# Ten weight slots with the expert loop written out, and expert 0's rows picked on TensorE, in a two-layer mixture-of-experts decoder

## The chip, the core and the metric

The kernel runs on one core of a Trainium2 chip. The metric is the device time of one execution in microseconds (us); the median of three executions is quoted. The engines are TensorE (PE; weight loads are listed as PEld), VectorE (DVE), ScalarE (ACT), GpSimd (POOL) and SyncE (SP). A name with a q behind it (SPq, ACTq) is that engine's sequencer issuing a DMA.

## What is computed

520 tokens (512 of a prompt, 8 decode tokens) of width 1024 pass two layers. Each layer has a mixer (short gated convolution in layer 0, RG-LRU recurrence in layer 1), a layer norm, a mixture of 32 experts in 4 groups, and a second layer norm. All is float32. The part around the change is the mixture:

```python
def hier_moe(x, w_group, w_expert, w_gate, w_up, w_down):
    gp = jax.nn.softmax((x2 @ w_group), axis=-1)
    g = jnp.argmax(gp, axis=-1)                        # one group of 4 per token
    el = (x2 @ w_expert).reshape(t, N_GROUPS, EXP_PER_GROUP)
    el = jnp.take_along_axis(el, g[:, None, None], axis=1)[:, 0]
    vals, idx = lax.top_k(softmax(el), TOP_K)          # two experts of its 8
    ...
    hmid = jax.nn.silu(xb @ w_gate[e]) * (xb @ w_up[e])
    out = hmid @ w_down[e]
```

Every expert's three matrices (1024x512, 1024x512, 512x1024) are read once per layer: 192 units of 2 MB, some 400 MB in all.

## The kernel before

**Weights.** `ring` holds RING = 9 slots of 2 MB. Every load has a position: 0 to 7 are layer 0's input weights, 8 and 9 its output weights, 10 to 105 its experts (gate, up and down of expert e at 10+3e, 11+3e, 12+3e), and so on for layer 1. Position p goes into slot p % RING. SP issues the loads in order (L427; L421 and L423 for the one unit that is loaded in two halves); ahead of each, `room(pos)` waits on the semaphore `freed` until the unit RING positions earlier has been used. PE raises `freed` in `project` (gate's first use, which releases the down unit before it, and its last), and with the first transposition of `turn_rows` (up's slot). For expert 0 the gate slot is released in two halves.

**Experts.** An expert handles up to 64 token rows; further rows go into overflow blocks after expert 30. PE per expert: `project(0)` with gate and `project(1)` with up (L894, 32 matmul instructions each), `turn_rows` for the next expert's rows (L880), `turn_hidden` (L916), `down` (L926, 16 instructions). A float32 matmul is two instructions. ACT applies Silu (L1208) and copies the result out (L1213); DVE multiplies (L1665), copies the turned hidden rows (L1668) and applies the norm's gain and bias to the turned token rows (L1646, L1649). POOL gathers each expert's token rows out of `x1` in DRAM with an indirect DMA (L567) into one of UNROLL = 3 buffers `xg`, and scatters the results to `yrows` (L574) from one of three buffers `yo`. The first HEAD = 6 experts and the last two are written out; the 24 between run in a loop of 8 trips of 3 on SP, PE, ACT.

**Routing, before expert 0.** The order in a layer is: the mixer's last products (L726), the logits (L778, L825), turned to tokens (L833); tokens turned to rows (`turn_token`, L787); DVE computes the variance and the logits, picks the group (L1546 to L1551), then twice the best expert (L1555 to L1561), and writes `picked` (L1562). Meanwhile ACT normalises the five token tiles `xk` (L1192), and ACT and POOL store them to `x1` (L1187, L558). PE counts ranks (L842, L845), DVE makes the one-hots `rowhot` (L1575), PE turns them into row numbers (L855), DVE writes `idx` (L1287), POOL gathers expert 0's rows (L567). PE sums the destinations (`destinations`, L863), runs six products as a warm-up (`warm`, L650) and waits for the gather; then `turn_rows`, DVE's `first_rows` (L1657, L1661), and `project(0)` of expert 0. `overflow` on DVE (blocks of experts with over 64 rows) follows `first_rows`.

**After the experts.** SP reads the scattered rows back into the ring slots of expert 30 (`rows_back`, L437), DVE and PE add them, the second layer norm follows, and layer 1 begins with its input weights (L444).

## Time and profile before

| | us |
|---|---|
| median of 3 executions (1460.77 to 1463.67) | 1462.91 |
| profiled execution, span from first to last instruction | 1458.7 |
| PE busy in it | 1295.1 (89%) |
| DVE busy | 467.0 (32%) |
| ACT busy | 204.4 (14%) |
| POOL busy | 145.9 (10%) |
| DMA moved | 475.39 MB, mean 326 GB/s |

The profile page has a row for each engine and resource in 40 equal slices of the span (36.5 us each). A chain of work follows the last instruction back to what released it at each step. A busy PE is not PE at its peak, since the ends of pipelined matmuls are modelled; so the question at each stretch is which wait ended last.

### The profile page before, as it was taken

How to read it: one execution, taken by the hardware profiler on the slowest of the kernel's cores; microseconds unless marked ns; L12 is line 12 of the kernel's file. 1: busy time of each engine (PE TensorE's matmuls, PEld its weight loads, DVE VectorE, ACT ScalarE, POOL GpSimd, SP SyncE). 2: the span in 40 equal slices, each digit the busy share in tenths (PEclk: the TensorE clock that was granted, in tenths of full speed). 3: DMA queues.
4: the chain of work that ended last, by engine and by line, in shares of the span. 5: the costliest groups of instructions: out<-in, count | busy, mean ns of one | idle time of the engine just before them, and what ended most of it. 6: DMA issues, size and time to landing. Idle time of an engine off the chain costs nothing.

```text
span 1458.7 us, 20116 instructions
## 1 busy us (share of the span) xinstructions
PE 1295.1 (89%) x8446; PEld 888.8 (61%) x8446; DVE 467.0 (32%) x966; ACT 204.4 (14%) x332; POOL 145.9 (10%) x165
## 2 busy tenths in 40 slices
PE   7999997999998878878899999989999878878886
PEld 6888876666664444444478887766666444444452
DVE  5666414322321111111245755261232111111116
ACT  1000012001000000000155563120100000000011
POOL 0000001111111111110000000021111111111101
PEclk9999998999999999999999999989999999999999
DMA  9930363899999999999995113269999999999995
GB/s 271 311 144 0 136 270 117 331 424 424 422 424 427 423 424 426 423 425 426 385 323 231 58 59 141 93 233 425 424 421 424 425 422 427 424 424 427 422 400 203
DMA packets 101037, 475.39 MB, mean 326 GB/s; under 512 B 18902, under 2 KB 53718, under 8 KB 66669
## 3 DMA queue, kind: packets, MB, share of 16 engines
q1 hardware_dynamic: 81869, 449.74, 76.2%
q0 software_dynamic: 14688, 18.58, 3.7%
q10 hardware_dynamic: 4424, 6.30, 1.6%
q8 instruction: 38, 0.62, 0.2%
q14 instruction: 18, 0.15, 0.0%
HBM read 480.31 MB, written 27.32 MB: 348 GB/s over the span
## 4 chain that ended last, share of the span: by engine, by line
PE 57%; DMA 36%; DVE 3%; issue 2%; ACT 1%; POOL 0%; SPq 0%; POOLq 0%; DVEq 0%
DMA ring<-in_moe_w_gate 29%; PE ps L894 15%; PE ps L685 9%; PE ps L626 9%; PE ps L926 7%; PE ps L726 7%; DMA ring<-in_moe_w_down 5%; PE ps L880 2%; PE ps L778 1%; PE ps L744 1%; DMA ring<-in_a_w_in 1%; PE ps L908 1%; PE ps L916 1%; PE ps L1017 1%; PE ps L863 1%
## 5 line engine op out<-in xcount | busy, mean ns | idle before, releaser
L894 PE MATMUL ps<-ring,A 128*64 128x256 f32 x4096 | 464.0, 381 | 85.2 <-DMA ring<-in_moe_w_up 53.3
L894 PEld LDWEIGHTS ps<-ring,A 128*64 128x64 f32 x4096 | 316.0, 137 | 251.1 <-issue 82.8
L926 PE MATMUL ps<-ring,C 128*64 128x512 f32 x1024 | 235.5, 601 | 38.3 <-DMA ring<-in_moe_w_down 15.2
L1665 DVE TENSOR_TENSOR C<-C,ps 128x256 f32<-128x256 f32 x64 | 27.0, 421 | 690.3 <-ACT C L1208 690.3
L926 PEld LDWEIGHTS ps<-ring,C 128*64 128x64 f32 x1024 | 78.6, 137 | 151.1 <-issue 131.5
L626 PE MATMUL ps<-A,ring 128*128 128x260 f32 x576 | 130.5, 388 | 3.3 <-DMA ring<-in_a_w_in 3.3
L626 PEld LDWEIGHTS ps<-A,ring 128*128 128x128 f32 x576 | 111.0, 193 | 20.9 <-issue 3.4
L726 PE MATMUL ps<-Bt,ring 128*128 128x260 f32 x512 | 116.1, 385 | 1.0 <-ACT C L1125 0.8
L567 POOL DMA_INDIRECT A<-x,idx x64 | 65.2, 1019 | 464.2 <-PE ps L880 448.6
L726 PEld LDWEIGHTS ps<-Bt,ring 128*128 128x128 f32 x512 | 96.1, 190 | 20.1 <-DVE A L1490 2.5
L1208 ACT ACTIVATE C<-ps 128x256 f32<-128x256 f32 x64 | 24.6, 384 | 525.7 <-PE ps L894 493.1
L880 PEld LDWEIGHTS ps<-ident,A 128*128 128x128 f32 x512 | 62.5, 194 | 23.8 <-issue 23.8
L880 PE MATMUL ps<-ident,A 128*128 128x128 f32 x512 | 74.2, 288 | 0.0
L685 PE MATMUL ps<-A,ring 128*128 128x260 f32 x264 | 61.6, 382 | 0.0
L685 PEld LDWEIGHTS ps<-A,ring 128*128 128x128 f32 x264 | 50.2, 190 | 7.7
L555 POOL TENSOR_TENSOR stat<-stat,half_neg 104x5 f32<-104x5 f32 x2 | 2.4, 1186 | 437.0 <-DVE stat L1287 437.0
L1649 DVE TENSOR_TENSOR A<-A,gb 128x512 f32<-128x512 f32 x62 | 42.9, 692 | 2.1
L1646 DVE TENSOR_TENSOR A<-ps,gb 128x512 f32<-128x512 f32 x62 | 42.2, 681 | 0.0
L1668 DVE COPY C<-ps 128x256 f32<-128x256 f32 x64 | 27.2, 425 | 42.5 <-PE ps L916 42.5
L1490 DVE SCALAR_TENSOR_TENSOR A<-A,ps 128x520 f32<-128x520 f32 x16 | 11.1, 696 | 89.3 <-PE ps L726 89.3
L1399 DVE TENSOR_TENSOR C<-C,ps 128x260 f32<-128x260 f32 x61 | 25.9, 425 | 41.3 <-PE ps L685 37.4
L574 POOL DMA_INDIRECT yrows<-A,Bt x22 | 22.5, 1021 | 125.0 <-ACT A L1213 119.0
(247 smaller groups left out, 978.8 us busy)
## 6 DMA issues: line engine op xcount, KB each, us to landing
ring<-in_moe_w_up SPq DMA_DIRECT2D x64, 2048.0 KB, 40.6
ring<-in_moe_w_down SPq DMA_DIRECT2D x64, 2048.0 KB, 39.6
ring<-in_moe_w_gate SPq DMA_DIRECT2D x62, 2048.0 KB, 41.4
ring<-in_a_w_in SPq DMA_DIRECT2D x24, 512.0 KB, 7.5
ring<-yrows SPq DMA_DIRECT2D x10, 1024.0 KB, 9.5
ring<-in_b_w_in SPq DMA_DIRECT2D x8, 1024.0 KB, 12.6
yrows<-C SPq DMA_DIRECT2D x5, 832.0 KB
ring<-in_a_w_out SPq DMA_DIRECT2D x2, 2048.0 KB, 12.3
```

The costliest lines, as they stand in the source:

```text
L567: pool.indirect_dma_start(out=xg[e % UNROLL], out_offset=None, in_=x1_dram[l], in_offset=bass.IndirectOffsetOnAxis(ap=idx[:, e:e + 1], axi ...
L626: mm = pe.matmul(bank, lhs(k), rhs(k), start=(k == 0), stop=(k == KT - 1))
L685: mm = pe.matmul(ps[:, part_bank(u, i), :HALF], w[:, k, :], x[i][:, k, :] if i in x else pieces[4 * t[i] + k], start=(k == 0), stop=(k == ...
L726: mm = pe.matmul(ps[:, 2 * PAIR[m] + hf, :HALF], ring[:, s, col:col + P], hT[:, k, hf * HALF:(hf + 1) * HALF], start=(k == 0), stop=(k == ...
L880: mm = pe.transpose(ps[:, k // 4, (k % 4) * P:(k % 4 + 1) * P], xv[:, k, :], ident[:, :])
L894: mm = pe.matmul(ps[hf * ROWS:(hf + 1) * ROWS, 3, u * FH:(u + 1) * FH], xgT[:, k, :], ring[:, slot, col:col + FH], start=(k == 0), stop=(k ...
L926: mm = pe.matmul(ps[nh * ROWS:(nh + 1) * ROWS, 2, :], hidT[:, at:at + ROWS], ring[:, slot, m * D + nh * 512:m * D + (nh + 1) * 512], start ...
L1399: tt(dst, x, y_, ALU.add).then_inc(ev_b[0], 1)
L1646: tt(xgT.rearrange("p k (h q) -> p k h q", h=2), turned[:, :, :, 0, :], gb[:, 2 * l, :].unsqueeze(2).unsqueeze(3).broadcast_to([P, KT, 2, ...
L1649: tt(xgT, xgT, gb[:, 2 * l + 1, :].unsqueeze(2).broadcast_to([P, KT, ROWS]), ALU.add).then_inc(ready, 1)
L1665: tt(gated, gated, ps[:, 3, FH:2 * FH], ALU.mult).then_inc(ready, 1)
L1668: dve.tensor_copy(hidT, ps[:, 4, :FT * ROWS]).then_inc(ready, 1)
```

## The change

Two things in one kernel. First, RING is 10 and the expert loop is written out on SP, PE, ACT for all 32 experts. [...]

Second, expert 0's rows are no longer gathered. DVE finds early which tokens pick expert 0 (group 0 is the best group, and fewer than two of the group's other experts have a larger logit), PE ranks them with five small products, DVE makes a one-hot `slots0`, and PE multiplies it with the normalised tiles `xk` into bank 6. ACT copies that out, PE transposes four blocks, ACT applies gain and bias into `xgT`. The row numbers of the other experts (`row_numbers`) are computed in the middle of expert 0's `project(0)`, `destinations` after its `project(1)`; `overflow` on DVE comes after expert 0; the warm-up is gone. The wait for the next expert's gather stands behind `project(1)`, not ahead of it.

```diff
-RING = 9
+RING = 10
...
-UNROLL = 3
-HEAD = 2 * UNROLL
+OUT_BUFS = 3
+IN_BUFS = 2
...
-        C = sb("C", [P, 6 * D])
+        C = sb("C", [P, NT * D + TT])
...
-        zeros = C[:TT, 5 * D + 256:5 * D + 768]
+        zeros = ring[:TT, ring_slot(POS_OUT[0] + 1), :512]
...
+        picked0 = sb("picked0", [TT, NT], BF16)
+        above0 = key[:, :, :EPG - 1]
+        slots0 = rowover[:, :NT, :]
...
-        xg = [A[:, i * D:(i + 1) * D] for i in range(UNROLL)]
+        xg = [A[:, i * D:(i + 1) * D] for i in range(IN_BUFS)]
+        rows0 = xg[0][:, :D // 2]
...
-        gated = C[:, 5 * D:5 * D + FH]
-        hidT = C[:, 5 * D + FH:5 * D + FH + FT * ROWS]
-        yo = [A[:, 3 * D + KT * ROWS:4 * D], Bt[:, 7 * 512:8 * 512], C[:, 5 * D + 512:6 * D]]
+        gated = A[:, 2 * D:2 * D + FH]
+        hidT = A[:, 2 * D + FH:2 * D + FH + FT * ROWS]
+        yo = [A[:, 3 * D + KT * ROWS:4 * D], Bt[:, 7 * 512:8 * 512], A[:, 2 * D + 512:3 * D]]
...
-                        if m == KT // 2 - 1:
-                            sp.wait_ge(sq2_ok, NT)
                         input_unit1(m)
                     pos = POS_IN[1] + KT // 2
                     room(pos)
+                    sp.wait_ge(sq2_ok, NT)
...
+                    if l == 0 and u == 1:
+                        sp.wait_ge(zero_ok, 1)
+                        for i in range(NT + 1):
+                            n_ = TT if i < NT else P - TT
+                            sp.dma_start(rows_dram[i * TT:i * TT + n_].rearrange("t k (h n) -> t (k h) n", h=2),
+                                         zeros[:n_].unsqueeze(1).broadcast_to([n_, 2 * TOPK, 512])).then_inc(zero_out, 16)
+                        sp.wait_ge(zero_out, 16 * (NT + 1))
...
-                for e in range(HEAD):
-                    expert(l, POS_EXP[l] + 3 * e, e)
-                with sp.Fori(0, TRIPS) as i:
-                    for j in range(UNROLL):
-                        expert(l, POS_EXP[l] + 3 * (HEAD + j), i * UNROLL + (HEAD + j), i * (3 * UNROLL))
-                for e in (*TAIL, END):
+                for e in range(NE):
...
-                    if e >= UNROLL:
-                        pool.wait_ge(t_mm[l], e - UNROLL + 2)
+                    if e >= IN_BUFS:
+                        pool.wait_ge(t_mm[l], e - IN_BUFS + 2)
                     pool.indirect_dma_start(
-                        out=xg[e % UNROLL], out_offset=None, in_=x1_dram[l],
+                        out=xg[e % IN_BUFS], out_offset=None, in_=x1_dram[l],
                         in_offset=bass.IndirectOffsetOnAxis(ap=idx[:, e:e + 1], axis=0),
                         bounds_check=T - 1, oob_is_err=False,
...
-                for e in range(END + UNROLL + 1):
-                    if e < NE:
+                for e in range(END + OUT_BUFS + 1):
+                    if 0 < e < NE:
                         gather(e)
-                    if e == UNROLL + 1:
+                    if e == OUT_BUFS + 1:
                         pool.wait_ge(idx_ok[l], 2)
                         pool.wait_ge(zero_out, 16 * (NT + 1))
-                    if e > UNROLL:
-                        d = e - UNROLL - 1
+                    if e > OUT_BUFS:
+                        d = e - OUT_BUFS - 1
                         pool.wait_ge(y_act[l], d + 1)
-                        scatter(yo[d % UNROLL], dest[:, d:d + 1], y_out[d % UNROLL])
+                        scatter(yo[d % OUT_BUFS], dest[:, d:d + 1], y_out[d % OUT_BUFS])
                 pool.wait_ge(idx_ok[l], 3)
...
-                for i in range(1, NT):
+                for i in range(1, NT - 1):
                     turn_token(i)
-
+                pe.wait_ge(expert0_dve, 2 * l + 1)
+                pe.matmul(ps[:TT, 7, 256:256 + NT], before[:, :], picked0[:, :], start=True, stop=False)
+                for j in range(NT - 1):
+                    mm = pe.matmul(ps[:TT, 7, 256 + j + 1:256 + NT], ones[:, :],
+                                   picked0[:, j:j + 1].broadcast_to([TT, NT - 1 - j]), start=False, stop=(j == NT - 2))
+                mm.then_inc(expert0_mm, 1)
+                turn_token(NT - 1)
+
+                pe.wait_ge(expert0_dve, 2 * l + 2)
+                for i in range(NT):
+                    pe.wait_ge(xn_done, 2 * NT * l + i + 1)
+                    xv = xk[i].rearrange("r (p q h b) -> r h q p b", q=2, h=2, b=2)
+                    for h in range(2):
+                        mm = pe.matmul(ps[h * ROWS:(h + 1) * ROWS, 6, :], slots0[:, i, :], xv[:, h],
+                                       start=(i == 0), stop=(i == NT - 1))
+                mm.then_inc(expert0_mm, 1)
 
                 pe.wait_ge(pick_ok, l + 1)
...
-                pe.wait_ge(xn_done, 2 * NT * l + NT)
-                for c in range(TOPK * NT):
-                    if c % NT == 0:
-                        pe.wait_ge(hot_ok, 4 * l + c // NT + 1)
-                    for h in range(2):
-                        mm = pe.matmul(ps[h * ROWS:h * ROWS + Q, 5, :NE], rowhot[:, c, h * Q:(h + 1) * Q],
-                                       ohtok[:, c // NT, c % NT, :], start=(c == 0), stop=(c == TOPK * NT - 1))
-                mm.then_inc(idx_mm, 1)
+                for q in range(2):
+                    pe.wait_ge(rows0_ok, 2 * l + q + 1)
+                    rv = rows0[:, q * 256:(q + 1) * 256].rearrange("r (p b) -> r b p", b=2)
+                    for b in range(2):
+                        mm = pe.transpose(ps[:, q, b * P:(b + 1) * P], rv[:, b, :], ident[:, :])
+                    mm.then_inc(t_mm[l], 1)
+
+                def row_numbers():
+                    for c in range(TOPK * NT):
+                        if c % NT == 0:
+                            pe.wait_ge(hot_ok, 4 * l + c // NT + 1)
+                        for h in range(2):
+                            mm = pe.matmul(ps[h * ROWS:h * ROWS + Q, 5, :NE], rowhot[:, c, h * Q:(h + 1) * Q],
+                                           ohtok[:, c // NT, c % NT, :], start=(c == 0), stop=(c == TOPK * NT - 1))
+                    mm.then_inc(idx_mm, 1)
...
+                            if k:
+                                row_numbers()
...
-                    pe.wait_ge(loaded[slots[0]], load_target(pos) + trip * 16)
-                    project(0, slots[0], True, first=(e0 == 0))
-                    pe.wait_ge(loaded[slots[1]], load_target(pos + 1) + trip * 16)
-                    b = (e0 + 1) % UNROLL
+                    pe.wait_ge(loaded[slots[0]], load_target(pos))
+                    project(0, slots[0], True, first=(e == 0))
+                    pe.wait_ge(loaded[slots[1]], load_target(pos + 1))
+                    b = (e + 1) % IN_BUFS
+                    project(1, slots[1], False).then_inc(gu_mm[l], 1)
+                    if e == 0:
+                        destinations()
                     if more:
-                        pe.wait_ge(gath[UNROLL * l + b], 16 * ((e0 + 1) // UNROLL + 1) + trip * 16)
-                    project(1, slots[1], False).then_inc(gu_mm[l], 1)
+                        pe.wait_ge(gath[IN_BUFS * l + b], 16 * ((e + 1) // IN_BUFS + (b > 0)))
...
-                destinations()
-                warm(WARM // 2)
-                pe.wait_ge(gath[UNROLL * l], 16)
-                turn_rows(xg[0], t_mm[l], halves=True)
-                for e in range(HEAD):
-                    expert(e, e, sums_too=(e == SUMS))
+                for e in range(END):
+                    expert(e, sums_too=(e == SUMS))
                     if e == TURN_END:
                         turn_end()
                     if e == SPREAD:
                         pe.wait_ge(endT_ok, l + 1)
                         spread_norm(l, R_G1 + l, R_B1 + l)
-                with pe.Fori(0, TRIPS) as i:
...
+                act.wait_ge(expert0_mm, 2 * l + 2)
+                for q in range(2):
+                    act.activation(rows0[:, q * 256:(q + 1) * 256], ps[:, 6, q * 256:(q + 1) * 256], ACT.Copy
+                                   ).then_inc(rows0_ok, 1)
+                for q in range(2):
+                    act.wait_ge(t_mm[l], q + 1)
+                    for h in range(2):
+                        for b in range(2):
+                            k, at = 4 * q + 2 * h + b, b * P + h * ROWS
+                            ins = act.activation(xgT[:, k, :], ps[:, q, at:at + ROWS], ACT.Identity,
+                                                 bias=gb[:, 2 * l + 1, k:k + 1], scale=gb[:, 2 * l, k:k + 1])
+                    ins.then_inc(t_sb[l], 1)
+
+                act.wait_ge(gaps_ok, 2 * l + 2)
+                act.activation(gex, gsh, ACT.Exp).then_inc(exp_ok, 1)
+                act.activation(s5[:, 8, :], s5[:, 7, :], ACT.Exp).then_inc(exp_ok, 1)
                 step(act.activation(gated[:TT, :1], half_neg[:, :1], ACT.Silu))
...
+                step(tt(above0, el[:, :, 1:EPG], over(el[:, :, 0], EPG - 1), ALU.is_gt))
+                tt(v5(12), gl[:, :, 0], v5(0), ALU.is_equal)
+                step(dve.tensor_reduce(v5(11), above0, AX, ALU.add))
+                stt(picked0[:, :], v5(11), float(TOPK), v5(12), ALU.is_lt, ALU.mult).then_inc(expert0_dve, 1)
...
+                dve.wait_ge(expert0_mm, 2 * l + 1)
+                step(stt(v5(13), ps[:TT, 7, 256:256 + NT], 1.0, picked0[:, :], ALU.add, ALU.mult))
+                stt(slots0, slotno[:, :].unsqueeze(1).broadcast_to([TT, NT, ROWS]), 1.0, over(v5(13), ROWS),
+                    ALU.add, ALU.is_equal).then_inc(expert0_dve, 1)
...
-                first_rows()
-                overflow()
                 for e in range(END):
                     expert(e)
                     if e == 0:
+                        overflow()
...
-    nc = bacc.Bacc("TRN2", target_bir_lowering=False, num_devices=1)
+    nc = bacc.Bacc("TRN2", target_bir_lowering=False, num_devices=1, dynamic_dma_scratch_size=4096)
```

## Rows read from the trace of the kernel before

**Rows 1.** The page: GB/s moved, in 40 equal slices of the span.

```profile
GB/s 271 311 144 0 136 270 117 331 424 424 422 424 427 423 424 426 423 425 426 385 323 231 58 59 141 93 233 425 424 421 424 425 422 427 424 424 427 422 400 203
```

**Rows 2.** The chain in order of time: start us, length us, what; experts.

```profile
258.85 7.13 PE ps L894 x64
...
271.68 6.91 PE ps L894 x64
...
284.23 6.91 PE ps L894 x64
...
480.71 42.31 DMA ring<-in_moe_w_gate
```

**Rows 3.** SP's queue in order of time: start us, length us, engine, line, transfer.

```profile
233.43 0.38 SPq L427 DMA_DIRECT2D ring<-in_moe_w_down  x1
260.82 0.33 SPq L421 DMA_DIRECT2D ring<-in_moe_w_gate  x1
262.55 0.33 SPq L423 DMA_DIRECT2D ring<-in_moe_w_gate  x1
266.31 0.33 SPq L427 DMA_DIRECT2D ring<-in_moe_w_up  x1
...
967.22 0.33 SPq L421 DMA_DIRECT2D ring<-in_moe_w_gate  x1
```

**Rows 4.** Stretches: length, each engine's busy us, PEclk, DMA share, GB/s.

```profile
260.82:290.00 29.18, 28.05 (x220) 19.35 (x218) 9.46 (x23) 1.96 (x4) 4.10 (x4) 1.00 0.96 372
967.22:1000.00 32.78, 31.09 (x241) 21.44 (x239) 10.88 (x26) 2.35 (x5) 4.69 (x5) 1.00 0.98 382
440.00:680.00 240.00, 192.76 (x1384) 111.17 (x1385) 33.75 (x63) 15.32 (x31) 31.66 (x31) 1.00 1.01 424
```

**Rows 5.** Timeline of layer 0's routing: start us, length us, engine, line, op, tiles.

```profile
241.32 0.18 DVE L1546 TENSOR_REDUCE Bt<-Bt 104x5 f32<-104x20 f32 x1
...
245.06 1.21 ACT L1192 ACTIVATE C<-ps,stat 104x1024 f32<-104x1024 f32 x1
...
246.68 0.33 DVE L1562 TENSOR_TENSOR picked<-Bt 104x160 bf16<-104x160 f32 x1
...
247.06 0.40 PE L842 MATMUL ps<-picked,before 104*104 104x192 bf16 x1 [2.49 <-DVE picked L1562]
...
247.92 0.22 ACT L1199 ACTIVATE Bt<-Bt 104x20 f32<-104x20 f32 x1 [1.64 <-DVE Bt L1566]
...
248.98 0.89 DVE L1575 TENSOR_TENSOR Bt<-Bt,slotno 104x320 f32<-104x320 f32 x2
...
249.61 1.28 PE L855 MATMUL ps<-Bt 104*32 104x32 f32 x40 [1.72 <-DVE Bt L1575]
...
253.31 1.10 POOL L567 DMA_INDIRECT A<-x,idx  x1 [7.24 <-DMA x<-C]
...
254.31 2.93 PE L650 MATMUL ps<-ident 128*128 128x128 f32 x12
...
268.02 3.65 PE L926 MATMUL ps<-ring,C 128*64 128x512 f32 x16 [0.56 <-issue]
```

**Rows 6.** Stretches of 1 us, columns as in 4: where PEclk changes.

```profile
243.00:244.00 1.00, 0.98 (x8) 0.94 (x8) 0.90 (x4) 1.00 (x2) 0.69 (x1) 0.76 0.76 160
...
257.00:258.00 1.00, 1.00 (x10) 0.96 (x8) 0.18 (x1) 0.00 (x0) 0.02 (x1) 0.91 0.42 90
...
953.00:954.00 1.00, 0.63 (x6) 0.63 (x6) 0.93 (x4) 1.00 (x1) 0.00 (x0) 0.75 0.83 242
```

**Rows 7.** POOL's gathers (L567): one in 252:254, one in 280:281.

```profile
DMA to landing us min/median/max: 2.9/2.9/2.9
...
DMA to landing us min/median/max: 10.7/10.7/10.7
```

**Rows 8.** The page: the queues that carry instructions.

```profile
q8 instruction: 38, 0.62, 0.2%
q14 instruction: 18, 0.15, 0.0%
```

## What is expected of the change, and why

> **What bounds the kernel now.** I read the GB/s line first [rows 1]. Two plateaus near 424 GB/s stand in it, slices 9 to 19 and 28 to 38: the experts' weights. Ahead of each the line falls towards zero: the ring is full and the stream waits for PE. The chain of waits then says who ends last inside a plateau. In layer 0 it is PE at first: expert 0 starts at 258.85, the next two at 271.68 and 284.23, so PE needs 12.55 us for an expert [rows 2]. Later the chain goes through the gate load's 42.31 us [rows 2]: PE has eaten its lead and waits for the stream. In 440 to 680 us the core moves 424 GB/s while POOL issues 31 indirect DMAs, a gather and a scatter for each expert [rows 4]: 15.5 us for an expert, 2.9 more than PE needs. So a layer ends when the stream has delivered its last unit. Two things alone can move that: how many units lie in the ring before the stream stops, and when it starts again. PE's work in the plateau, and the loop's branches, cost nothing.
>
> SP's queue shows the stop [rows 3]. The last unit that fits is asked for at 233.43, the next at 260.82, when the first half of expert 0's gate has been used. It goes on at 262.55 (other half) and 266.31 (up's slot). In layer 1 the first such issue is at 967.22, so everything there is 706.4 us later. The restart is not clean: from 260.82 to 290.00 the core moved 372 GB/s [rows 4], that is 10.86 MB, which takes 25.6 us at 424; in effect the stream restarts at 264.4. In layer 1 it is 382 over 32.78 us [rows 4]: 29.5 us, in effect 970.5.
>
> **The tenth slot.** One more unit, 2.097 MB, is loaded while the line is near zero [rows 1] (slices 7 and 26, before the routing, have room), and is missing from the plateau: 2.097 MB / 424 GB/s = 4.95 us a layer, 9.9 in all. The ends: 0 if something other than the stream were last, 9.9 if it is; the second, since the chain lies on the loads [rows 2].
>
> **The early pick, at full clock, in layer 0's times.** DVE's reduction at 241.32 takes 0.18 [rows 5]. Four more such operations follow it, one overlapped: 0.75. Then PE's five small products lie beside DVE's group search; a PSUM operation (0.2) and the one-hot over 104x320 (half of L1575's 0.89, so 0.45 [rows 5]) come behind the wait: 0.85 with a semaphore. So slots0 stands at about 244.4, and `picked`, written at 246.68 to 247.01 [rows 5], comes 1.6 us later, 248.6; all of the routing is queued behind these.
>
> PE's one-hot products are ten of 512 columns, 20 instructions. `down` has the same form, 16 in 3.65 us [rows 5], 0.228 each: 4.6 us from 245.1 (after the last token tile is turned) to 249.7. The last tile `xk` is there at 245.06 + 1.21 = 246.3 [rows 5], in time. The rank products wait behind them, not for `picked`: 0.85 from L842's 247.06 to DVE's next step [rows 5], so 250.5. Transposes 0.4, then four ACT operations on 64 columns, each 0.22 as the small one [rows 5] (not over 0.25): `project(0)` starts at 251.9, against 258.85.
>
> Its first half takes 1.75 (a quarter of 7.13 [rows 2]), so the first slot half is free at 253.7. Then `row_numbers`, 1.28 [rows 5], and the second half: 256.7. `project(1)` ends at 260.2, `destinations`, twice the width, 1.3: 261.5. Here PE waits for the gather of expert 1, which is new at this place, and behind it in PE's order stand the release of up's slot, `turn_hidden` and `down`. Row numbers end at 250.89 now and the gather starts at 253.31 [rows 5]: 2.4. With 1.1 for the issue [rows 5] and 2.9 to landing [rows 7] (the 2.9 includes part of the issue; the sum is an upper end) that is at most 255.0 + 6.4 = 261.4, just in time. The other end of its price is the landing in a full stream, 10.7 us [rows 7]: 269, 7.6 late. I take the first, since the gate slot's load of 2.1 MB has mostly been moved by then and the queue is empty until up's slot is free; 10.7 goes into a rival. Up's slot is free at 261.7 against 266.31, expert 1 starts at 267.3 against 271.68.
>
> Until then gate and up, 4.2 MB, have been moved, 9.9 us' worth; with rows and the slow start of each issue, as in the restart before, the stream in effect restarts at 258.2 to 258.7: a gain of 5.7 to 6.2.
>
> **At low clock.** [...] Nothing in the change fills PE before 243, so I leave the fall where it is. Warm-up L650 and the products before it are what preceded its rise; after the change the one-hot products do that work, from 245.1. [...] If the clock is back after some 5 us of them, 11 are slow and 9 fast: 252.1 instead of 249.7, and all of the list slips by 2.4 us: the gain in layer 0 is 5.7 less 2.4, plus 0.4 because the gate slot's load then runs into up's without a gap: 3.7. In layer 1 the fall comes within 953 to 954 [rows 6], which is 247 in layer 0's times, in a stretch where PE waited for `picked` and now has the one-hot products. So I take the full clock there: 5.7. Together 9.4. The ends are 0 and 12.4.
>
> **What the trace does not show.** The written-out loops must be fetched. The page has 0.62 and 0.15 MB of instructions [rows 8], for 20116 executed less the repeats. An expert has some 187 (2894 in 15.5 experts [rows 4]); 42 executed experts were repeats, 7850 instructions. The other 12300 made 0.77 MB, so 0.49 MB more: 1.2 us at 424 GB/s, 2.3 by the share of that queue (0.2% of 1458.7 for 0.62 MB). I take 1.6. A stall of PE for a fetch has 2.9 us an expert as cover, and the six experts that are already written out run at 12.55 [rows 2]. Below zero it can't go.
>
> The zero writes of 4.4 MB with SP waiting behind them (10.5 us at 424) go ahead of position 9, into slices 2 to 4, of which the fourth is at 0 [rows 1]: nothing. Two gather buffers: the gather is asked for two experts (31 us) ahead of its use, against 10.7 [rows 7]; the scatter now stands behind a gather that waits half an expert longer, and its buffer is wanted two experts later: nothing. `overflow` comes after expert 0 on DVE, whose work of all kinds from 260.82 to 290.00 is 9.46 us [rows 4], so it fits before expert 1's Silu: nothing. The `sq2_ok` wait in layer 1 moves from the fourth input unit to the gate weights, which PE wants after two channels: nothing.
>
> [...]
>
> **Sum.** 9.9 + 9.4 - 1.6 = 17.7 us, from a span of 1458.7: 1441.0. The median of the runs, 1462.91, stands 4.2 above the span; the same 4.2 is added: 1445.2.
>
> **Rivals.** (a) The slot pays and the pick does not: expert 1's gather lands as in the full stream, 7.6 late, and `down`'s slot with it. For it speaks the 10.7 [rows 7], against it the empty queue. 7.6 a layer is more than the pick gives in either (3.7 and 5.7), but the queue then starts full, so I put the pick at nothing: 1458.7 - 9.9 + 1.6 + 4.2 = 1454.6. [...]
> (b) The clock stays high in both layers and the restart is clean: the upper end, 12.4: 1442.2; with nothing lost to fetches 1440.6. For it: PE has more to do in the routing. Against it: the fall at 243 comes before.
> (c) The change does not do what it says for one part: the slot's extra unit is not loaded before the stop, or PE becomes the bound. Against: 2.9 us of slack. It leaves 17.7 - 9.9: 1455.1.
> (d) Slower: POOL's DMAs wait for each other in the smaller area. POOL would then need for each expert gather and scatter one after the other, between 10.7 + 2.9 + 2.2 of issue = 15.8 and 2 x (10.7 + 1.1) = 23.6 us [rows 5, 7]; it decides above 15.5 [rows 4]. Over 62 experts that is 19 to 500 us: 1464 to 1950, the slot and the pick lost behind it. For it: the area is set small, and nothing in the trace shows what is enough. Against: with 10.7 us to land [rows 7] and two issues in 15.5 us [rows 4], no more than two are in flight.
>
> **How the numbers follow.** Forecast 0.62 (1442 to 1449), (a) 0.16, (b) 0.12, (c) 0.04, (d) 0.06. The range 1440 to 1455 takes in (a), (b) and the unknown costs, and leaves out (d) and parts of (a) and (c). What a measurement of this kernel can tell from no change is about 0.2%, 2.9 us. Faster: 0.91, from all but (d) and a share of (a) and (c) with further losses (0.03); slower 0.06.
>
> **What would show it.** Right: SP's issue after the stop at 253.9 to 256.3 and 960 to 961; ten units between stop and restart; about 15.5 us an expert in the plateau as now; the chain through the gate loads, sooner than 435 us. Wrong: a wait of PE for `A<-x` behind `project(1)` of expert 0 (a); one-hot products much over 4.6 us in layer 1 (the clock); POOL's issues spaced like landings (d); GB/s in the plateau below 424 (instruction fetches).

## The result, and the profile after

The kernel after takes 1452.99 us (median of four executions, 1450.00 to 1453.19), beside 1461.84 for the kernel before on the same chip (1459.66 to 1463.67): ratio 0.9934, 95% interval 0.9921 to 0.9947. It is faster by some 9.6 us, and was predicted to be so by 17.7. (A ratio is not the quotient of the two medians; here and below they differ by up to 0.0016, and differences are worked out from ratios, times 1461.8. Each is uncertain by some 2 us.) The profiled execution is the quickest of the four: span 1448.2, against 1458.7 before; the other three took 1452.8 to 1453.2, so what is read from this one profile can be some 3 us better than the median.

The page: the span, the GB/s in 40 slices, and the queues that carry instructions (packets, MB, share).

```profile
span 1448.2 us, 19523 instructions
...
GB/s 268 301 220 0 112 296 117 326 423 421 423 425 422 424 425 424 422 425 423 377 317 306 59 59 123 109 261 422 423 424 422 422 425 424 422 426 423 422 379 194
...
q8 instruction: 68, 1.11, 0.3%
q14 instruction: 20, 0.16, 0.0%
```

Against [rows 1], slices 3 and 22 have grown (144 to 220 and 231 to 306): the tenth slot is filled there. The plateaus stand at the same height. Against [rows 8], 30 packets of 16 KB more are fetched on q8.

SP's queue behind the stops, and the weight loads it asks for:

```profile
254.07 0.33 SPq L424 DMA_DIRECT2D ring<-in_moe_w_up  x1
256.72 0.33 SPq L426 DMA_DIRECT2D ring<-in_moe_w_up  x1
264.03 0.38 SPq L430 DMA_DIRECT2D ring<-in_moe_w_down  x1
271.13 0.33 SPq L430 DMA_DIRECT2D ring<-in_moe_w_gate  x1
...
954.95 0.33 SPq L424 DMA_DIRECT2D ring<-in_moe_w_up  x1
957.59 0.33 SPq L426 DMA_DIRECT2D ring<-in_moe_w_up  x1
963.99 0.38 SPq L430 DMA_DIRECT2D ring<-in_moe_w_down  x1
```

The first answers to 260.82 in [rows 3]: 6.75 us sooner. But 7.3 us lie between the second and the third issue, where there were 3.8 before. TensorE's timeline says what it waits for there (start, length, what; in brackets the idle time ahead of it and who ended it), in layer 0, and in its last two lines in layer 1:

```profile
244.83 4.80 PE L851 MATMUL ps<-C,Bt 104*64 104x512 f32 x20
...
252.10 1.95 PE L915 MATMUL ps<-ring,A 128*64 128x256 f32 x16 [1.20 <-ACT A L1221]
253.97 0.82 PE L876 MATMUL ps<-Bt 104*32 104x32 f32 x40
254.73 5.40 PE L915 MATMUL ps<-ring,A 128*64 128x256 f32 x48
259.96 1.31 PE L884 MATMUL ps<-Bt 104*64 104x32 f32 x40
263.62 1.16 PE L901 MATMUL ps<-ident,A 128*128 128x128 f32 x8 [2.35 <-DMA A<-x,idx]
264.62 0.40 PE L937 MATMUL ps<-ident,A 128*128 128x128 f32 x2
265.58 5.10 PE L947 MATMUL ps<-ring,A 128*64 128x512 f32 x16 [0.56 <-issue]
...
945.70 4.80 PE L851 MATMUL ps<-C,Bt 104*64 104x512 f32 x20
...
963.58 1.16 PE L901 MATMUL ps<-ident,A 128*128 128x128 f32 x8 [1.44 <-DMA A<-x,idx]
```

The one-hot products (L851) and `project(0)` of expert 0 stand where they were predicted. Then PE waits for expert 1's rows, 2.35 us in layer 0 and 1.44 in layer 1, with the release of a slot (the first of L901) and `down` behind that wait. The chain of waits holds the gather itself:

```profile
256.25 7.32 DMA A<-x,idx
263.57 0.04 issue
263.62 1.16 PE ps L901 x8
```

Stretches, with the columns of [rows 4]: behind the restarts, the plateau, the place where PEclk had fallen before, where the stream runs dry, and where PEclk has fallen now.

```profile
254.07:300.00 45.93, 41.89 (x376) 27.29 (x378) 16.60 (x50) 3.72 (x8) 7.18 (x7) 0.96 0.89 351
954.95:1000.00 45.05, 41.91 (x390) 28.82 (x391) 16.56 (x50) 5.11 (x11) 7.16 (x7) 1.00 0.93 369
440.00:680.00 240.00, 193.78 (x1410) 115.95 (x1408) 32.06 (x60) 15.32 (x31) 32.19 (x32) 1.00 1.01 424
...
243.00:244.00 1.00, 1.00 (x15) 1.00 (x13) 0.86 (x5) 1.00 (x2) 0.00 (x0) 1.00 0.51 119
...
262.00:265.00 3.00, 1.38 (x10) 1.21 (x10) 0.00 (x0) 0.00 (x0) 0.00 (x0) 1.00 0.03 8
...
266.00:267.00 1.00, 1.00 (x4) 0.26 (x2) 0.93 (x4) 0.00 (x0) 0.54 (x1) 0.50 0.89 360
```

For 3 us the core moves 8 GB/s: the two halves that were asked for at 254.07 and 256.72 are in (the last part recorded lands at 263.4), and the next load is asked for at 264.03. By the prediction's own measure (what the stretch moved, at 424 GB/s) the stream in effect restarts at 254.07 + 45.93 x (1 - 351/424) = 262.0 and at 954.95 + 45.05 x (1 - 369/424) = 960.8, against 264.4 and 970.5 before.

What comes out at the ends is in three rows: `down` of expert 30 in layer 0, and PE in the last expert of layer 1.

```profile
699.14 3.65 PE L947 MATMUL ps<-ring,A 128*64 128x512 f32 x16 [0.56 <-DMA ring<-in_moe_w_down]
...
1408.90 4.54 PE L915 MATMUL ps<-ring,A 128*64 128x256 f32 x40 [2.02 <-issue]
...
1415.45 3.65 PE L947 MATMUL ps<-ring,A 128*64 128x512 f32 x16 [0.56 <-issue]
```

The same in the kernel before:

```profile
703.82 3.65 PE L926 MATMUL ps<-ring,C 128*64 128x512 f32 x16 [0.56 <-DMA ring<-in_moe_w_down]
...
1425.36 3.65 PE L926 MATMUL ps<-ring,C 128*64 128x512 f32 x16 [0.56 <-issue]
```

Layer 0 ends 4.7 us sooner, the whole 9.9. That doesn't add up to what the parts gave. In layer 0 the restart came 2.4 sooner and the slot is worth 4.95: 7.35, of which 4.7 is left, so 2.65 went in the plateau. In layer 1 the restart came 9.7 sooner, with the slot 14.65, and 9.9 is left: 4.75 lost, of which 2.02 is the stall in the middle of the last expert's products, where PE waits for no semaphore ("issue"). So by these two profiles 7.4 us are lost behind the restarts (two single executions, and those of one kernel differ by some 3 us). In the profiles the plateau moved its 424 GB/s all the time; what takes them is the question for the experiments.

### The profile page after: what moved, and what is told of

The parts are those of the page before. It is cut to its first block, busy times and chain, and to the rows that moved or that the text cites. A ratio compares the mean times of both kernels' runs of the same rounds, so it can differ in the third digit from the quotient of the medians.

```text
span 1448.2 us, 19523 instructions
## 1 busy us (share of the span) xinstructions
PE 1294.0 (89%) x8464; PEld 895.6 (62%) x8464; DVE 465.9 (32%) x970; ACT 210.4 (15%) x352; POOL 151.9 (10%) x163
## 4 chain that ended last, share of the span: by engine, by line
PE 42%; DMA 35%; issue 2%; DVE 2%; ACT 1%; POOL 0%; POOLq 0%; DVEq 0%; SPq 0%
DMA ring<-in_moe_w_up 15%; PE ps L915 15%; DMA ring<-in_moe_w_gate 15%; PE ps L947 8%; PE ps L625 8%; PE ps L725 3%; DMA ring<-in_moe_w_down 3%; PE ps L901 2%; PE ps L743 1%; DMA A<-x,idx 1%; PE ps L929 1%; PE ps L937 1%; PE ps L1031 1%; PE ps L777 1%; DMA yrows<-A,Bt 0%
## 5 line engine op out<-in xcount | busy, mean ns | idle before, releaser
L915 PEld LDWEIGHTS ps<-ring,A 128*64 128x64 f32 x4096 | 326.0, 137 | 235.9 <-issue 74.9
L947 PE MATMUL ps<-ring,A 128*64 128x512 f32 x1024 | 238.3, 606 | 39.6 <-issue 24.4
L1680 DVE TENSOR_TENSOR A<-A,ps 128x256 f32<-128x256 f32 x64 | 26.9, 421 | 673.4 <-ACT A L1233 673.4
L947 PEld LDWEIGHTS ps<-ring,A 128*64 128x64 f32 x1024 | 81.3, 139 | 152.0 <-issue 127.6
L1233 ACT ACTIVATE A<-ps 128x256 f32<-128x256 f32 x64 | 24.6, 384 | 497.0 <-PE ps L915 487.7
L901 PEld LDWEIGHTS ps<-ident,A 128*128 128x128 f32 x496 | 60.1, 194 | 27.1 <-issue 23.1
L901 PE MATMUL ps<-ident,A 128*128 128x128 f32 x496 | 71.9, 288 | 3.8 <-DMA A<-x,idx 3.8
L1238 ACT ACTIVATE A<-ps 128x512 f32<-128x512 f32 x42 | 25.1, 597 | 238.5 <-PE ps L947 238.5
L573 POOL DMA_INDIRECT yrows<-A,Bt x42 | 49.0, 1167 | 69.6 <-ACT A L1238 57.9
L1683 DVE COPY A<-ps 128x256 f32<-128x256 f32 x64 | 27.2, 425 | 50.7 <-PE ps L937 50.7
L1510 DVE SCALAR_TENSOR_TENSOR A<-A,ps 128x520 f32<-128x520 f32 x16 | 11.1, 696 | 89.3 <-PE ps L725 89.3
```

The source lines that it names most:

```text
L573: pool.indirect_dma_start(out=half_rows, out_offset=bass.IndirectOffsetOnAxis(ap=where, axis=0), in_=rows, in_offset=None, bounds_check=2 ...
L901: mm = pe.transpose(ps[:, k // 4, (k % 4) * P:(k % 4 + 1) * P], xv[:, k, :], ident[:, :])
L915: mm = pe.matmul(ps[hf * ROWS:(hf + 1) * ROWS, 3, u * FH:(u + 1) * FH], xgT[:, k, :], ring[:, slot, col:col + FH], start=(k == 0), stop=(k ...
L947: mm = pe.matmul(ps[nh * ROWS:(nh + 1) * ROWS, 2, :], hidT[:, at:at + ROWS], ring[:, slot, m * D + nh * 512:m * D + (nh + 1) * 512], start ...
L1680: tt(gated, gated, ps[:, 3, FH:2 * FH], ALU.mult).then_inc(ready, 1)
L1683: dve.tensor_copy(hidT, ps[:, 4, :FT * ROWS]).then_inc(ready, 1)
```

## The experiments

My theory: the slot gives its 9.9; the pick gives less than its 9.4, because the new wait for the gather holds a slot and `down`; and the code of the written-out loops costs more than the 1.6 of the prediction. The rival: writing out costs what was said or nothing, and the slot or the pick gives less (a transfer that was hidden anyway).

**One part at a time.** Three kernels, with the one before on the same chip.

a_written_out: the kernel before, loops written out on SP, PE and ACT, nothing else.

```diff
-                for e in range(HEAD):
+                for e in range(END):
                     expert(e, e, sums_too=(e == SUMS))
...
-                with pe.Fori(0, TRIPS) as i:
-                    for j in range(UNROLL):
-                        expert(i * UNROLL + (HEAD + j), HEAD + j, i)
-                for e in TAIL:
-                    expert(e, e)
...
```

> The kernel before with its expert loops written out, nothing else. Theory (the ledger of the two traces): instruction fetches take time from the stream of weights in each plateau, some 2 us a layer, so +4: 1465.8 against 1461.8. The prediction's own term was +1.6: 1463.4. Rival: writing out costs nothing: 1461.8.

Measured: 1467.46, ratio 1.0048 (1.0035 to 1.0061), 7.0 us slower, more than any of the three figures expected.

b_nine_slots: the kernel after with nine slots (`C`, `zeros` and the `sq2_ok` wait as before).

```diff
-RING = 10
+RING = 9
...
```

> The changed kernel with nine weight slots (loops written out and the early pick kept; one buffer back in its old place). Theory: it lacks 2.1 MB of prefetch in each layer, 4.95 us each, so 1453.0 + 9.9 = 1462.9, about the time of the kernel before. Rival, the slot pays only about half in the changed kernel because of a slower plateau: 1458.

Measured: 1461.25, ratio 0.9997 (0.9989 to 1.0006).

c_slot_no_pick: ten slots, written out, expert 0 gathered as before (the edit against the kernel before, in parts).

```diff
-RING = 9
+RING = 10
...
-        xg = [A[:, i * D:(i + 1) * D] for i in range(UNROLL)]
+        xg = [A[:, i * D:(i + 1) * D] for i in range(IN_BUFS)]
...
-                for e in range(HEAD):
+                for e in range(END):
...
```

> Ten slots and written-out loops, but expert 0's rows are gathered as in the kernel before, with first_rows and the warm-up. Theory: the pick is worth 7 to 8 us in the two layers together (the stream restarts in effect 3.0 and 4.9 earlier), so 1460.5. The prediction had 9.4 for it: 1462.4. Rival (the new wait for expert 1's gather eats the pick): 1454.

Measured: 1456.39, ratio 0.9970 (0.9959 to 0.9980), between the expected 1460.5 and the rival's 1454.

With these the parts can be read in two orders. Slot: from b to after 0.0063, 9.2 us; from a to c 0.0078, 11.4. Pick: from a to b 0.0051, 7.5 us; from c to after 0.0036, 5.3. Writing out: 7.0. The slot is as predicted, the pick gives 5 to 8 instead of 9.4, and the code costs four times what I took. The rival that writing out costs 1.6 or nothing falls; that the pick gives less is true besides.

**The wait for expert 1's rows.** f_down_first is the kernel after with another order in expert 0: up's slot is released by the first product of `destinations`, then come `turn_hidden` and `down`, and only then the wait for the gather and `turn_rows`.

```diff
+                            if free and c == 0 and h == 0:
+                                mm.then_inc(freed, 1)
...
                     if e == 0:
                         destinations()
-                    if more:
+                    def next_rows():
                         pe.wait_ge(gath[IN_BUFS * l + b], 16 * ((e + 1) // IN_BUFS + (b > 0)))
-                    if more:
                         turn_rows(xg[b], t_mm[l], True)
+
+                    if more and e > 0:
+                        next_rows()
...
                     down(slots[2], y_mm[l])
+                    if e == 0:
+                        next_rows()
```

> The changed kernel with another order in expert 0: up's slot is released by the first product of the destinations, then come turn_hidden and down, and only then the wait for expert 1's gather and turn_rows, whose first transposition releases down's slot. Theory (the loss at the restart is down's slot waiting behind the gather): the slot is free 4.5 us earlier in layer 0 and 2 us in layer 1, so 1453.0 - 6.5 = 1446.5. Rival: the gather is not what limits the restart, and the time stays at 1453.

Measured: 1446.83, ratio 0.9915 (0.9900 to 0.9930); a second time (f_again) 1447.66, 0.9904 (0.9891 to 0.9918).

> The kernel f_down_first once more, beside j_pe_loop on the same chip: ratio to the kernel before 0.9915 within 0.0015, 1447 us.

Its SP queue and timeline in layer 0:

```profile
261.31 0.38 SPq L430 DMA_DIRECT2D ring<-in_moe_w_down  x1
267.32 0.33 SPq L430 DMA_DIRECT2D ring<-in_moe_w_gate  x1
```

```profile
263.33 3.65 PE L950 MATMUL ps<-ring,A 128*64 128x512 f32 x16 [0.56 <-issue]
266.92 1.16 PE L903 MATMUL ps<-ident,A 128*128 128x128 f32 x8
269.62 5.62 PE L917 MATMUL ps<-ring,A 128*64 128x256 f32 x50 [1.55 <-DVE A L1684]
```

The third issue goes out 3.5 us behind the second (257.78), not 7.3; `down` takes 3.65 us instead of 5.10, with the granted clock at 1.00 instead of 0.50 to 0.73; and the gather is in before it is wanted. (The clock fell there in the three profiles with PE's wait for the gather in layer 0, those of after, b_nine_slots and k_pe_loop6 below, and in none of the four without it.) So the wait of 2.35 and 1.44 us is what cut the pick: 3 to 4 us come back when the slots are released and `down` is run ahead of it. The edit does these together, and what each gives was not tried apart. This kernel beats both.

```diff
-    nc = bacc.Bacc("TRN2", target_bir_lowering=False, num_devices=1)
+    nc = bacc.Bacc("TRN2", target_bir_lowering=False, num_devices=1, dynamic_dma_scratch_size=4096)
```

> [...] My theory: nothing, ratio 1.000 within 0.001 (1461.6 us), since in the kernel after the issues on POOL were not spaced like the landings. The rival of the prediction, that POOL's DMAs wait for each other in the smaller area: 1464 us or more, and the gathers of expert 1 to 4 issued further apart than in the kernel before.

Measured: 1460.80, ratio 0.9998 (0.9989 to 1.0007). It costs nothing here, and rival (d) is out. POOL issues its first gathers 1.41, 1.31 and 3.01 us apart, as in the kernel before (1.41, 1.30, 2.90).

**What does written-out code cost by?** Two theories were left: PE stalls for its own code, as in the 2.02 us above; or the fetches lie on the queues of the weights and make the loads late. The second can be had without PE: h2_more_code is the kernel before, all loops as they were, with idle DVE given 100 fills of one element, written out, in 19 experts of each layer. DVE's idle time there, ahead of its next multiplication, is 12.7 us in the kernel before; a fill takes 59 ns.

```diff
+                    if SPREAD + NT < e < END - 1:
+                        for q in range(100):
+                            dve.memset(ps[0:1, 7, q:q + 1], 0.0)
```

> The kernel before (PE, ACT and SP looped) with 100 one-element fills on DVE behind its last operation in each of the experts 11 to 29 of both layers, written out: 3800 instructions of 64 bytes, 0.24 MB, some 15 more instruction packets of 16 KB. DVE stands idle for some 10 us at that place in each expert, and PE's code and work are unchanged. In the traces so far the last of the 16 parts of a weight load lands 7.0 to 9.0 us after the first at the end of the streams of the kernel before, and 8.7 to 10.6 us in the written-out ones; one instruction packet lies 1.07 us on its queue. Theory 1: code that is fetched on the queues which the weights fill makes the slowest of them later, and every weight load with it. 30 packets more cost 5.9 us by a_written_out, so 15 cost some 3 us: 1464.7 us, and the spread of the parts at the ends of the streams is wider by 1 to 2 us. Theory 2: writing out costs what TensorE waits for its own code: nothing here, 1461.6 us within 1. Theory 3: fetches for DVE go over other queues than those for PE, or spread evenly over all sixteen: under 1 us, while the packets rise all the same.

Measured: 1484.53, ratio 1.0156 (1.0142 to 1.0170): 23 us, far more than any of the three theories gave. Since that was so much, the fills themselves had to be ruled out. h3_loop_fills has the same 100 fills at the same places from a loop of ten.

```diff
+                        with dve.Fori(0, 10) as i:
+                            for q in range(10):
+                                fill = dve.memset(ps[0:1, 7, q:q + 1], 0.0)
+                            fill.then_inc(filled, 1)
+                            dve.wait_ge(filled, i + (10 * k + 1))
```

> The control for h2_more_code: the same 100 one-element fills on DVE at the same place of the same 19 experts of each layer, executed from a small loop of ten fills (ten trips, with a wait for their own count at the end of each), so that DVE does the work and hardly any code is added. h2_more_code took 1.0156 of the kernel before, and in it one of the 16 parts of every weight load falls 0.9 to 1.1 us further behind with each instruction packet of 8 KB. If that code is what costs: ratio 1.000 within 0.0015 (1461.5 us), at most 3 instruction packets more than the kernel before, and the last part of the loads within 10 us of the first. If the fills themselves cost (DVE busy, their writes): 1470 us or more, as in h2_more_code.

Measured: 1461.83, ratio 0.9998 (0.9988 to 1.0009), with 4 packets more than the kernel before, where I had said 3 at most. The work costs nothing; its code, fetched while the weights stream, costs 23 us. The instruction queues of h2_more_code, then those of h3_loop_fills:

```profile
q8 instruction: 38, 0.62, 0.2%
q14 instruction: 47, 0.39, 0.1%
```

```profile
q8 instruction: 38, 0.62, 0.2%
q14 instruction: 22, 0.18, 0.0%
```

h2_more_code has 29 packets of 8 KB more than [rows 8], 0.24 MB (63 bytes for each of the 3800 fills), which are 0.6 us of a stream at 424 GB/s, and they cost 0.8 us each. Such a packet lies 0.33 us on its queue by the DMA records, so even the time on one queue, 9.6 us for 29, is less than half of the cost; where the rest goes no run here shows. In the plateau nothing is to be seen of that: 424 GB/s in 440 to 690, as in the kernel before. Two stretches of 5 us at the end of layer 0's stream in h2_more_code, and PE's rows at that time:

```profile
715.00:720.00 5.00, 4.44 (x28) 2.50 (x26) 2.14 (x4) 0.38 (x1) 0.00 (x0) 1.00 0.17 67
720.00:725.00 5.00, 4.94 (x40) 3.11 (x36) 0.00 (x0) 0.60 (x1) 0.98 (x1) 1.00 0.16 61
```

```profile
725.45 3.67 PE L894 MATMUL ps<-ring,A 128*64 128x256 f32 x32 [0.51 <-DMA ring<-in_moe_w_up]
...
731.13 3.65 PE L926 MATMUL ps<-ring,C 128*64 128x512 f32 x16 [0.56 <-DMA ring<-in_moe_w_down]
```

PE waits for weights while the 16 DMA engines are busy by 0.17. The landing records of the trace have 16 parts for each load, and show them singly: of the up load that PE waits for here the first lands at 704.84, the fifteenth at 713.05, the last at 725.40, and PE goes on at 725.45, with the last. Worked out from these records, for the 9 or 10 loads whose last part lands in a stretch of 50 us near the end of each stream (medians, us; "last two" is the time from the fifteenth part to the sixteenth):

| kernel | first to last, 650 to 700 | last two | first to last, 1350 to 1400 | last two |
|---|---|---|---|---|
| before | 8.9 | 0.5 | 7.1 | 0.0 |
| g_scratch | 7.5 | 0.7 | 6.6 | 0.0 |
| h3_loop_fills | 7.6 | 0.4 | 7.3 | 0.2 |
| a_written_out | 10.9 | 0.9 | 8.8 | 0.5 |
| b_nine_slots | 11.1 | 1.3 | 8.5 | 0.7 |
| after | 10.4 | 1.0 | 8.7 | 1.5 |
| h2_more_code | 18.1 | 10.7 | 16.0 | 8.7 |
| k_pe_loop6 (below) | 7.4 | 0.7 | 7.4 | 0.2 |
| j_pe_loop (below) | 12.0 | 1.8 | 11.5 | 2.4 |

In h2_more_code one part of every load is alone at the end, and the gap to the next steps from 5.9 to 6.8, 7.7, 8.5 and 9.4 us between loads that land at 565, 581, 598, 614 and 630, with one instruction packet fetched in each interval. The trace doesn't say which of the 16 DMA engines moves a part or a packet; but the gap rises only behind a packet, and one part alone falls behind each time, in both layers. From this I infer that DVE's code comes over one of the 16, always the same, and that every load waits for that one. That the other fifteen then run ahead into further slots is an inference as well: it fits the 424 GB/s of the plateau and a loss that shows only at the end of the stream.

PE's packets of 16 KB seem not to come all over the same one. In the kernel after the gap of the last two parts steps by 1.4 us at 575.0, with a packet of q8 at 572.1, and again by 1.4 at 1235.8, with one at 1233.0; behind the packet at 599.1 it shrinks from 2.4 to 0.9, as if another of the 16 had been hit, and behind the one at 616.1 it stays. The kernels with PE written out end their streams some 3 and 1.5 us wider than those with PE looped. In layer 0 that is of the size of the 2.65 us lost in the plateau, in layer 1 it is less than the 2.7. Which packet delayed which load was read only at these places, so for PE this share is an inference. The width alone is no price either: j_pe_loop below ends layer 1's stream 11.5 wide and its twin f_again 8.6, and the two are within noise of each other.

The other theory, PE standing for its own code, has a part too. The 2.02 us at 1406.88 in the kernel after begin as a packet of q8 starts (1406.6). The same stall in the last expert's products is 2.16 in b_nine_slots, 2.09 and 2.29 in f_down_first and f_again, 1.56 in j_pe_loop and 0.80 in a_written_out; c_slot_no_pick, written out too, has none over 0.7, nor has any kernel whose PE keeps a loop of three or six experts. How the cost divides between stalls and late loads was not measured.

**Can PE's code be had cheaper?** Two kernels put PE alone back into a loop. j_pe_loop is f_down_first with experts 10 to 29 as two trips of ten, the least with which ten slots and two gather buffers come round (here and below the counts in its waits change with the trip):

```diff
+                with pe.Fori(0, 2) as i:
+                    for j in range(10):
+                        expert(i * 10 + (10 + j), trip=i, e0=10 + j)
```

> f_down_first with a loop on PE only: experts 10 to 29 run as two trips of ten (ten slots and two gather buffers come round in ten experts), 180 x 10 x 2 instructions fewer in the program, 0.23 MB. Theory 1 (fetched code on the weights' queues): 14 packets fewer, and 2.5 to 3 us faster than f_down_first, near 1444 us, if a trip's second pass needs no new fetch. Rival: ten experts (115 KB of code) are fetched anew in each trip: packets as in f_down_first or more, and the time within 1 us of it or above.

Measured: 1449.05, ratio 0.9911 (0.9896 to 0.9927), as f_again beside it. The rival held: q8 has 72 packets, more than written out.

```profile
q8 instruction: 72, 1.18, 0.3%
```

k_pe_loop6 is b_nine_slots with experts 6 to 29 as four trips of six on PE.

```diff
+                with pe.Fori(0, 4) as i:
+                    for j in range(6):
+                        expert(i * 6 + (6 + j), trip=i, e0=6 + j)
```

> b_nine_slots (nine slots, early pick, all written out) with a loop on PE only: experts 6 to 29 as four trips of six (69 KB of code). j_pe_loop has shown that a body of ten experts (115 KB) is fetched anew on each trip (72 instruction packets against 68), and the kernel before that one of three (36 KB) is not (38). If six stay in the buffer: 18 experts a layer fewer, 0.41 MB, 25 packets fewer, and 4 to 5 us faster than b_nine_slots, ratio 0.9965 to the kernel before, 1456.5 us. If six don't stay: packets and time as in b_nine_slots, ratio 0.9997, 1461.2 us.

Measured: 1455.38, ratio 0.9958 (0.9944 to 0.9972), 5.7 us less than b_nine_slots, with 25 of the 68 packets gone:

```profile
q8 instruction: 43, 0.70, 0.2%
```

So a body of six experts (some 70 KB) is not fetched anew on its trips (43 packets), one of ten (some 120 KB) is (72, against 68 written out). Both sizes are estimates from the 30 packets of 16 KB that the 42 experts written out add, 11.7 KB for an expert. And PE's code is most of what writing out costs: 5.7 of the 7.0 us, each uncertain by some 2; the kernel that branches is the faster one.

m_loop6_down_first puts f_down_first's order into k_pe_loop6.

> k_pe_loop6 (nine slots, early pick, PE in trips of six experts) with the edit of f_down_first. If the parts add up: k_pe_loop6's ratio of 0.9958 less the 0.0019 to 0.0030 that the edit gave with ten slots (0.9934 to 0.9915 and 0.9904), 1451 to 1452.5 us, still above f_down_first's 1447. Rival: with nine slots the queue of weight loads is the shorter, the loads freed early are worth more, and PE's loop fetches 25 packets less: 1447 us or less, as good as f_down_first.

Measured: 1447.76, ratio 0.9900 (0.9883 to 0.9917). I had expected the parts to add up, and missed: the edit is worth 8.5 us here, against 3 to 4 with ten slots. In layer 0 the third and fourth issue behind the stop go out at 258.44 and 264.46, in k_pe_loop6 at 262.57 and 270.93: 4.1 and 6.5 us sooner, where f_down_first gained 2.7 and 3.8 on the kernel after. Whether that is all of it I haven't measured. So nine slots with the early pick, `down` first and PE in a loop of six are as fast as ten slots written out, which can't be looped as shortly.

## Why the prediction was right or wrong

**The time: in the range, not at the sum.** The measured 1453.0 lies in 1440 to 1455, but 7.8 us above the 1445.2 and outside the 1442 to 1449 that had the 0.62; the ratio puts the gain at 9.6 instead of 17.7 us. It falls near the 1454.6 of rival (a), mostly for another reason than (a)'s. That the range held is owed to its width and to two terms of the pick that offset each other in part, and is in that measure luck.

**What bounds the kernel: right.** Both ends stay on the weight stream. The chain lies on the loads, and the kernels with a slot more gain 9.2 to 11.4 us.

**The tenth slot, 9.9: right.** 9.2 measured between b_nine_slots and after, 11.4 between a and c.

**The early pick, 9.4: the order of steps right, the size not.** `picked` came at 248.62 (predicted 248.6) and `project(0)` at 252.10 (251.9), the first issue at 254.07, all near the steps. But the two causes behind it came out against each other.

The low clock was priced too high. In the profile of the kernel after, the products of 512 columns took 4.80 us for 20 in both layers, at full clock, so the 2.4 us were not paid: PEclk is 1.00 in 243 to 244, where it had fallen to 0.76 before [rows 6], on the way to 0.50 in 244 to 257. The 2.4 us, eleven of the 20 products slow, are a term that no run shows. In five of the seven profiles of kernels with the pick PEclk was at 0.50 somewhere in 242 to 246 of layer 0, and it cost little: the 20 products took 4.95 to 5.78 us there, against 7.0 (4.6 and the 2.4) in the prediction; in b_nine_slots the clock is back before 247, some 2 us behind the first of the products at 244.66, where I had taken 5. So the kernel after was lucky in its profile, by up to some 1 us. b_nine_slots has the longest:

```profile
244.00:245.00 1.00, 1.00 (x6) 0.59 (x6) 0.90 (x5) 1.00 (x2) 0.11 (x1) 0.50 0.80 283
...
244.66 5.78 PE L853 MATMUL ps<-C,Bt 104*64 104x512 f32 x20
```

The step that failed is the gather of expert 1. I had the row numbers done at 255.0 and the gather issued 2.4 later, at 257.4, with 1.1 and 2.9 to its landing at 261.4, "just in time". The row numbers were done at 254.8 and the gather was issued at 256.25, sooner than that, but took 7.32 to where PE could go on, between the ends 2.9 and 10.7 of [rows 7]: it now lies beside the two halves that go into expert 0's gate slot, for which PE itself had just made room (254.07 and 256.72). A row of the kernel before had shown such a case, and the prediction didn't use it: the gather at 267.83, 1.5 us behind the issue at 266.31.

```profile
DMA to landing us min/median/max: 8.3/8.3/8.3
```

PE had to wait 2.35 us for expert 1's gather, the stream ran dry behind it, and behind PE's idle time the clock fell at another place: PEclk 0.50 in 266 to 267, `down` 5.10 us instead of 3.65. In effect the restart gained 2.4 us in layer 0 (3.7 predicted) and, in layer 1, 9.7 less the 4.7 of layer 0's end, 5.0 (5.7 predicted). The gather's wait was rival (a) at well under its size (2.35 and 1.44 us of waiting, not 7.6): 5.3 to 7.5 us of pick are left, not none.

**The instruction fetches, -1.6: mis-sized, -7.0.** This is most of the miss. The bytes were right (0.49 MB on q8). The step that failed is the price: I spread them over all sixteen engines (1.2 us) or took the queue's share (2.3), which on the page is a share of all sixteen as well, and gave PE's stalls the slack of the plateau as cover. What h2_more_code shows for DVE's code is that behind each packet one of a load's 16 parts falls 0.8 to 0.9 us further back (565 to 630), and PE waits for that part; for PE's own packets this is the likely reason, not a shown one. And the last expert of layer 1, at the end of the stream, had no such cover for its 2.02 us.

**Edits costed at nothing.** `dynamic_dma_scratch_size` at 4096 is shown to cost nothing (g_scratch, 0.9998). The zero writes, the two gather buffers, `overflow` and the moved `sq2_ok` wait were not tried apart; c_slot_no_pick holds all but `overflow` and shows no loss beyond the code's.

**The sum.** 9.2 + 7.5 - 7.0 = 9.7 in the order a, b, after, against 9.9 + 9.4 - 1.6. Of the 8 us between, 5.4 are the code, 1.9 the pick and 0.7 the slot. By the other order (a, c, after) the slot gives 11.4 and the pick 5.3, so the pick is 4.1 short and the slot 1.5 over; the runs don't divide it more finely.

**The signs.** First issue in layer 0: within the window given. In layer 1 954.95, below the 960 to 961 given: that window doesn't follow from the prediction's own terms. With layer 0 over 8.65 sooner (4.95 and 3.7) and the first issue 4.5 to 6.9 sooner behind it, 967.22 gives 951.7 to 954.1. Plateau expert, chain, and POOL's issues as said. Of the signs of being wrong the one for (a), a wait of PE for `A<-x` behind `project(1)`, did appear, in both layers. "GB/s below 424" would not have shown the fetches: the plateau of the kernel after stands at 424, as does that of h2_more_code, which is 23 us slower.

## What to carry to other kernels

When a stream of weights is the bound, don't price what is fetched beside it by its bytes or by its time on a queue: measure it. Both came out too low here: 0.24 MB of code for an idle engine, 0.6 us by its bytes and 9.6 by its packets' time, cost 23 us. Loop, engine by engine, what is not fetched anew on each trip (here six experts, not ten), before writing out for the sake of another slot. And when a change moves work ahead of a transfer, ask what stands behind the wait for that transfer: releasing the slots and running `down` first was worth as much as half the pick.

## What the runs showed of the hardware

- A loop body of six experts on PE, some 70 KB by an estimate, is not fetched again on its trips (k_pe_loop6, 43 packets on q8), one of ten, some 120 KB, is (j_pe_loop, 72, against 68 written out).
- 29 instruction packets of 8 KB for DVE, behind which always one part of a load falls back, cost 0.8 us each while the weights stream (h2_more_code, 23 us); 25 packets of 16 KB for PE, behind which it seems not always to be the same part (after, the packets at 572.1 and 599.1), cost 0.23 us each (b_nine_slots less k_pe_loop6, 5.7 us).
- The parts of a weight load drift apart in the stream, from 2 to 3 us between the first and the last at its start (280 to 330 us) to 6.6 to 8.9 at its end in the kernels without added code (before, g_scratch); why was not tried.
- A gather of one expert's rows landed 2.9 us after issue with no load under way (before, 253.31), 6.1 to 8.3 beside the first loads behind the stop (after, 256.25 to 257.66, and before, 267.83), 10.7 in the full stream (before, 280.46).
- The clock's fall in layer 0's routing differs between executions: PEclk is at 0.50 in part of 242 to 246 in five of the seven profiles with the pick and at 1.00 throughout in the other two (after, m_loop6_down_first), with the same products on PE. With the routing as it was before, it falls at 243.5 in one profile (before) and behind 248 in others (a_written_out, h3_loop_fills).
